# The gate_up weights of an expert in two transfers of 4 MB in place of four of 2 MB

## What is computed

```python
def moe_ffn(x, ...):
    xf = rmsnorm(x, norm_g).reshape(t, d)
    logits = xf @ w_router + b_router
    top_logits, top_idx = lax.top_k(logits, TOP_K)        # 4 of 32
    top_w = jax.nn.softmax(top_logits, axis=-1)
    ...
    def expert_block(args):
        xb, e = args
        gu = xb @ w_gate_up[e] + b_gate_up[e]             # 1024 x 2048
        gate = jnp.minimum(gu[:, 0::2], SWIGLU_LIMIT)
        up = jnp.clip(gu[:, 1::2], -SWIGLU_LIMIT, SWIGLU_LIMIT)
        hidden = (up + 1.0) * gate * jax.nn.sigmoid(SWIGLU_ALPHA * gate)
        return hidden @ w_down[e] + b_down[e]             # 1024 x 1024
```

## Time and profile before

| | |
|---|---|
| median of 3 runs | 2503.1 us |
| profiled execution, its own time | 2504.55 us |
| its span in the trace | 2502.3 us |
| mean granted clock of PE, share of full speed | 0.981 |
| busy: PE, weight loads of PE, VectorE, ScalarE, GpSimd | 96%, 88%, 43%, 23%, 13% |
| moved by DMA | 502.08 MB, mean 201 GB/s |
| SP's queue (q1): packets, MB, share of the 16 engines | 233888, 449.87, 51.6% |
| gate_up transfers | 128 of 2048 KB, 11.2 us from issue to landing |
| down transfers | 64 of 2048 KB, 8.8 us from issue to landing |

### The profile page before, as it was taken

The page is one execution under the profiler, slowest core; times in us unless marked ns, Lnnn a source line. Parts: engine busy times, 40 slices in busy tenths (PEclk is TensorE's granted clock), DMA queues, the critical chain, the costliest instruction groups (busy, mean ns, idle before and its releaser), DMA issues.

```text
span 2502.3 us, 43449 instructions
## 1 busy us (share of the span) xinstructions
PE 2407.9 (96%) x17425; PEld 2193.4 (88%) x17426; DVE 1086.8 (43%) x2423; ACT 567.4 (23%) x1034; POOL 330.3 (13%) x275
## 2 busy tenths in 40 slices
PE   6999999999996899999999999999999999999997
PEld 5878877444485899999999999999999999999997
DVE  6435437999834433323333332333333333333332
ACT  3242244777721111111111111111111111111111
POOL 1101002444300010001010100101001010010101
PEclk9999998999997999999999999999999999999999
DMA  4322321000236678877888887787788888788882
GB/s 156 103 75 68 100 70 68 1 1 1 84 127 211 222 227 285 268 223 255 279 268 287 280 280 246 255 288 252 256 287 264 292 274 261 251 263 292 275 284 45
DMA packets 250237, 502.08 MB, mean 201 GB/s; under 512 B 7884, under 2 KB 36592, under 8 KB 250112
## 3 DMA queue, kind: packets, MB, share of 16 engines
q1 hardware_dynamic: 233888, 449.87, 51.6%
q0 software_dynamic: 14912, 45.71, 9.2%
q10 hardware_dynamic: 1344, 5.14, 0.6%
HBM read 469.59 MB, written 31.10 MB: 200 GB/s over the span
## 4 chain that ended last, share of the span: by engine, by line
PE 91%; DVE 4%; issue 3%; DMA 1%; ACT 0%; POOL 0%; DVEq 0%; ACTq 0%; POOLq 0%
PE bank L1049 41%; PE bank L1060 18%; PE bank L810 12%; PE bank L920 3%; PE bank L905 3%; PE bank L1037 2%; DVE hx L1430 2%; PE bank L1008 2%; PE bank L892 1%; PE bank L952 1%; PE bank L954 1%; PE bank L953 1%; PE bank L1000 1%; PE bank L908 1%; PE bank L890 1%
## 5 line engine op out<-in xcount | busy, mean ns | idle before, releaser
L1049 PE MATMUL bank<-hx,ring 128*128 128x140 f32 (+1 forms) x8192 | 1036.4, 288 | 24.9 <-issue 15.5
L1049 PEld LDWEIGHTS bank<-hx,ring 128*128 128x128 f32 x8192 | 1020.7, 197 | 31.7 <-issue 30.6
L1060 PE MATMUL bank<-hx,ring 128*128 128x140 f32 (+1 forms) x4096 | 514.7, 287 | 0.0
L1060 PEld LDWEIGHTS bank<-hx,ring 128*128 128x128 f32 x4096 | 507.0, 190 | 0.0
L766 ACT ACTIVATE hx<-hx 128x168 f32<-128x168 f32 x256 | 87.9, 343 | 1449.6 <-DVE hx L1501 1449.6
L1501 DVE TENSOR_SCALAR hx<-bank,hx 128x168 f32<-128x168 f32 x256 | 100.4, 392 | 636.4 <-PE bank L1049 636.2
L1526 DVE TENSOR_SCALAR hx<-bank,hx 128x168 f32<-128x168 f32 x256 | 100.5, 393 | 353.8 <-PE bank L1060 353.8
L582 POOL DMA_INDIRECT out_x<-mix,hx x66 | 99.8, 1511 | 821.9 <-ACT mix L759 779.9
L561 POOL DMA_INDIRECT mix<-xn_scratch,hx x66 | 64.9, 984 | 719.4 <-DVE hx L1425 709.4
L556 POOL TENSOR_TENSOR work<-work 128x512 f32<-128x512 f32 (+3 forms) x96 | 105.5, 1099 | 140.2 <-DVE work L1276 133.3
L810 PE MATMUL bank<-hx_r,mix_r 128*128 128x512 f32 x480 | 116.0, 401 | 8.0 <-DVE hx_r L1143 8.0
(11 more groups left out here) (205 smaller groups left out, 2159.2 us busy)
## 6 DMA issues: line engine op xcount, KB each, us to landing
ring<-in_w_gate_up SPq DMA_DIRECT2D x128, 2048.0 KB, 11.2
ring<-in_w_down SPq DMA_DIRECT2D x64, 2048.0 KB, 8.8
mix<-in_w_in SPq DMA_DIRECT2D x14, 1024.0 KB, 5.0
work<-in_w_in SPq DMA_DIRECT2D x14, 1024.0 KB, 5.0
ring<-in_x SPq DMA_DIRECT2D x8, 512.0 KB, 8.4
hx<-in_w_out SPq DMA_DIRECT2D x1, 4096.0 KB, 12.6
work<-in_x ACTq DMA_DIRECT2D x8, 512.0 KB, 4.9
out_x<-work SPq DMA_DIRECT2D x8, 512.0 KB, 4.3
```

Source lines behind the costliest of these rows:

```text
L1049: mm = e.matmul(bank[f % 2][:, part * CAP:part * CAP + w], gu_ring[:, k, f * 256 + part:(f + 1) * 256:2], xT[:, k, 0:w], start=k == 0, sto ...
L1060: return e.matmul(bank[2 + j % 2][:, 0:w], dn_ring[:, k, j * P:(j + 1) * P], hid[:, k, 0:w], start=k == 0, stop=k == KD - 1)
```

## The change

`load_expert` and the first load at L506 move the gate_up weights in two halves of 1024 columns. A half is 4 MB, and its rows in HBM are 4 KB long. Half `c` of expert `n` waits until column block `4c + 3` of expert `n - 1` is done. There are two semaphores `gu_in` in place of four, and PE waits on them before `f` = 0 and 4. Nothing else changes.

```diff
--- before.py
+++ after.py
@@ -310,7 +310,7 @@
         bias_in = sem("bias_in")
         bias_tr = sem("bias_tr")
         bias_ok = sem("bias_ok")
-        gu_in = [sem(f"gu_in{c}") for c in range(4)]
+        gu_in = [sem(f"gu_in{c}") for c in range(2)]
         dn_in = [sem(f"dn_in{c}") for c in range(2)]
         l_hot = sem("l_hot")
         l_id = sem("l_id")
@@ -455,7 +455,7 @@
         xnr = xn_dram.rearrange("(i p) d -> i p d", p=P)
         win_r = w_in[0].rearrange("(k p) (c n) -> c p k n", p=P, n=SL)
         rope_r = rope.rearrange("p (a h n) -> h p a n", a=2, h=2)
-        gu_r = w_gate_up[0].rearrange("e (k p) (c n) -> e c p k n", p=P, n=512)
+        gu_r = w_gate_up[0].rearrange("e (k p) (c n) -> e c p k n", p=P, n=1024)
         dn_r = w_down[0].rearrange("e (k p) (c n) -> e c p k n", p=P, n=512)
 
 
@@ -502,13 +502,13 @@
                 e.wait_ge(e_norm, i + 1)
                 e.dma_start(xnr[i], xn2[:, i % 2]).then_inc(e_st[i % 2], 16)
             e.wait_ge(e_prj, 2 * NT)
-            for c in range(4):
-                e.dma_start(gu_ring[:, :, c * 512:(c + 1) * 512], gu_r[0, c]).then_inc(gu_in[c], 16)
+            for c in range(2):
+                e.dma_start(gu_ring[:, :, c * 1024:(c + 1) * 1024], gu_r[0, c]).then_inc(gu_in[c], 16)
 
             def load_expert(n, x_e):
-                for c in range(4):
-                    e.wait_ge(m_gu, n * 8 + (2 * c - 6))
-                    e.dma_start(gu_ring[:, :, c * 512:(c + 1) * 512], gu_r[x_e, c]).then_inc(gu_in[c], 16)
+                for c in range(2):
+                    e.wait_ge(m_gu, n * 8 + (4 * c - 4))
+                    e.dma_start(gu_ring[:, :, c * 1024:(c + 1) * 1024], gu_r[x_e, c]).then_inc(gu_in[c], 16)
                 for c in range(2):
                     e.wait_ge(m_dn, n * 8 + (4 * c - 4))
                     e.dma_start(dn_ring[:, :, c * 512:(c + 1) * 512], dn_r[x_e, c]).then_inc(dn_in[c], 16)
@@ -1041,8 +1041,8 @@
             def block_matmuls(n, w):
                 e.wait_ge(g_xT, n * 3 + 3)
                 for f in range(KD):
-                    if f % 2 == 0:
-                        e.wait_ge(gu_in[f // 2], n * 16 + 16)
+                    if f % 4 == 0:
+                        e.wait_ge(gu_in[f // 4], n * 16 + 16)
                     e.wait_ge(m_up, n * 8 + (f + 1))
                     for part in range(2):
                         for k in range(KD):
```

## The result

The changed kernel takes 2517.66 us (median of 5 runs, 2514.15 to 2518.28), against 2503.1 us before (5 runs): a ratio of 1.0058, 95% interval 1.0043 to 1.0073. It is slower by 14.6 us. The profiled execution took 2517.82 us with a span of 2515.6, which is 13.3 us more than the span of before. Every trace in this document is of one execution, so single stops may differ from execution to execution.

What follows compares the result with a forecast made beforehand. The prediction took TensorE (PE), busy 2407.9 of 2502.3 us, as the bound, with weights arriving in time. Code loading +6, lower clock +3 and start -2 gave +7 us, so 2510 us, range 2500 to 2540.

Steps and rivals of the forecast that it cites:

- rival A: The forecast itself: longer PE stops at the jumps between code copies, 2510 us, bounds 2501 to 2521; chance 0.42.
- Weights in time: Expert stage: later-issued gate_up halves still land 20 and 17 us before PE needs them, cost 0.
- Code loading, +6 us: Four PE jumps after wide experts: instruction packets meet a full weight queue, 1.5 us each (0 to 3.2), +6 us.
- The lower clock, +3 us: Matmuls after the four jumps: all pay 1.6 us for a lower PE clock, where two did before, +3 us.
- The start, -2 us: Before expert 0: fewer packets shorten PE's 6.98 us wait for the first gather, between 0 and -6.98, taken as -2.
- Rival B: Nothing reaches PE: code packets slip between, or rows go in 2 KB pieces; 2501 to 2504 us; chance 0.28.
- Rival C: Token gather late at L1008 in 26 narrow experts, 2 us each, about 2550 us, or 2516 to 2520; chance 0.22.
- Rival D: Faster: merging saves fixed transfer time, 5 us per pair, PE seeing only 6.98 us at the start; 2496 us; chance 0.08.

Runs made afterwards that it cites:

- e6: Kernel before with gate_up untouched, first w_down load issued after j = 5 in place of j = 3: 2516.97 us, ratio 1.0064.
- e1: Kernel before with its four gate_up quarters of 2 KB rows, issued at the two later moments of the change: 2516.96 us, ratio to before 1.0062.
- e2: Changed kernel (halves, 4 KB rows) with both w_down loads issued after j = 7: 2500.45 us, ratio to before 0.9999.
- e5: Kernel before (quarters) with both w_down loads issued after j = 7: 2496.8 us, ratio 0.9984.
- e7: e5 with the last two gate_up quarters of expert 0 issued only after the first gather has landed: 2495.37 us, ratio to before 0.9966.
- e8: e2 with the second gate_up half of expert 0 issued only after the first gather has landed: 2499.5 us, ratio to before 0.9992.

## Why the prediction was right, and where its terms were off

The forecast was 2510 us in a range of 2500 to 2540, slower being the likeliest sign; measured were 2517.66. The mechanism of rival A held at the jumps, which is the whole loss. Its size did not: the sum said +7 us, and it was +14.6 between the medians, +13.3 between the spans. All three terms were off in the same direction. The range held because it was wide, from 3 us below the kernel before to 37 above it.

- **Weights in time** (17 to 20 us to spare, cost 0): right. The 4 MB half landed after 12.7 us, where 12.6 was taken from w_out's row.
- **Code loading, +6 us**: the mechanism was right, the term too small. It measured +7.8, that is 1.96 us a jump where I took 1.5 as the middle between 0 and 3.2. The lower bound had no ground: no packet under load came in time. And the length of a packet, to which I had looked in the earlier trace rows (two beside each other, 2.0 us each), is not what counts. With the change the same two come one after the other and take 1.1 and 1.3 us, and the stop behind them is 5.68 as before. At the jump stops a packet takes 1.0 to 1.1 us under load and is late. So the value belonged in the upper half: e6, where weights flow over the whole stretch, gives 5.1 - 2.5 = 2.6.
- **The lower clock, +3 us**: it measured +5.5, the largest miss. All four stops are followed by slow matmuls, as taken. But I let each pay 1.6, and they paid 1.7 to 2.4. Stops of this length had no row of their own before. Nor does the price grow steadily with the stop: in the earlier trace rows 2.48 us cost nothing and 2.18 us cost 1.6, and in e6 stops of 5.32 and 4.91 us cost 1.5 each and one of 5.20 cost about 3. What the runs do show is how often it is paid. All 12 jump stops of 4.0 to 5.3 us (the change, e1, e6) have slow matmuls behind them, and 10 of the 20 of 1.9 to 2.7 us (before, e2, e5, e7, e8).
- **The start, -2 us**: wrong, it measured +0.3. SP was indeed held back less, but all 8 MB still had to pass before the gather. The weight queue ran dry in the same microsecond, just after 808 us, with four transfers and with two. L1008 began at 813.84 (813.52 before). Its wait fell from 6.98 to 3.94 us only because PE and the gather came later. From SP's issue of expert 0's weights to the gather it was 24.7 us in place of 22.3, and PE's granted clock from 783 to 794 us was 0.50 in place of 0.57. Quarters can have this too: e5 had 0.50 and 24.7 us, and e2, with halves, 0.77 and 20.6. That the clock makes the difference fits all eight traces with two copies, but no run was made for it. Fewer and longer packets moved nothing here; e7, which takes the second 4 MB out of the gather's way, did bring what I had looked for here.
- **The rest**: the last expert and the run's end gave back 1.1 us, which had no term, and the first two experts' matmuls cost 0.7.

Stops, clock, start, the first two experts and the end: 7.8 + 5.5 + 0.3 + 0.7 - 1.1 = 13.2 us, against 13.3 between the spans.

Rival B (nothing reaches PE) falls with the stops; a code packet does run beside weights (e1 above), but it starts late, 1.8 to 3.1 us later than the usual 1.6 us ahead of PE's last matmul. Rival C had a chance of 0.22, and its place was real but the gather stayed in time. Issued at 1602.16, the second gather was over by 1611.2, 9.0 us against 8.4, with L1008 at 1612.81. These are the queues from 1611.2 to 1612.81 us, with no packet of the gather left:

```profile
q1 hardware_dynamic: 156, 0.64, 101.3%
```

The pause in its rows did not double with packets of twice the size. In the earlier trace rows 355 weight packets of 2 KB pass in 2 us without one of the gather; with the change it is 2 us again, 1605 to 1607, with half as many packets of 4 KB and the same bytes:

```profile
q1 hardware_dynamic: 177, 0.72, 97.5%
```

So the flow in bytes decided, as I had taken it, and rival C's 2 us per expert did not come: the trace shows 0.6 us more for the gather and no wait. The Trainium skill has the rule that an engine drains a whole packet before it turns to the next queue (DMA: Bandwidth & Descriptors, Queues, rings and completion order). With the profile's packets taken for those of the rule the doubling was to be expected, and the trace does not bear that out; whether the rule means other packets no run shows. Of the 1.7 us to spare about 0.6 are used up. Rival D's 5 us per merged pair stayed hidden, as the chain said (e2).

## What to carry to other kernels

Before making a transfer larger or later, look at what else uses the DMA engines in the stretch that it then fills. Here all weights had 17 us to spare and the loss came from a 16 KB code packet that PE needs at each of four stops, and from the clock after each stop. Where a program branches between copies of long code, keep the queues quiet for the last few us before a likely jump back; moving a load that has slack to just after the boundary cost nothing and gained 4 us. Keeping bulk loads out of the way of a small transfer that is waited for brought the first expert forward by 3 us.

## What the runs showed of the hardware that I had not expected

- A code packet is hardly slowed by weight traffic but put off by it. Behind a full weight queue it took 1.0 to 1.1 us and started 1.8 to 3.1 us later than in a quiet one, although other weights still flowed beside it (e1). The mean jump stop went from 2.1 to 5.1 us (e5, e6) by this alone. What inside the DMA engines puts it off stays open.
- The small gather is put off in the same way at the start: with 8 MB ahead of it L1008 begins 9.2 us after its issue, with 4 MB out of the way 6.2 (before, e7).
- Doubling the rows to 4 KB left the flow and the sharing almost as they were: 2 us at full flow hold 0.73 MB in 355 packets before and 0.72 MB in 177 with the change. And e1 and the change, which differ in rows, transfer size and number of issues, are 0.7 us apart in time, inside both intervals.
- A stop of 2 us can already be followed by the lower clock, and one of 2.5 us need not be: see the 12 and 20 jump stops above. Before, from 2132 to 2142 us, behind a stop of 2.18 us, the granted clock was 0.83; from 1560 to 1570 us, behind one of 2.48 us, it was 1.00.
